# Hyena filter generation on quarters of the TensorE array, two projection weight tiles fetched at the end of the filter phase, and a signal of its own for the norm's product

## The reference

```python
hn = _rmsnorm(x, norm_mix_g[l])
proj = hn @ w_in[l]                       # columns lru_x | lru_gate | hyena v | x1 | x2
kf = _hyena_filters(seq, ...)             # two-sided filters, two orders, 512 channels
y_hy = _hyena(hy_u, ..., kf, hy_skip[l])  # two long convolutions by FFT
y_cat = concat(_rmsnorm(y_lru), _rmsnorm(y_hy)); x = x + y_cat @ w_out[l]
x = x + _hier_moe(_rmsnorm(x, norm_ffn_g[l]), ...)

def _hyena_filters(...):
    z = sin(ff1 * (feats @ fw1 + fb1)); z = sin(ff2 * (z @ fw2 + fb2))
    h = (z @ fw3).reshape(seq, 2, HY_ORDER, D_HY) * exp(-t * deltas)
    hf, hb = h[:, 0], h[:, 1]                       # forward and backward half
    k = concatenate([hf, zeros, hb[1:][::-1]])      # 4096 positions
    k = k / (sum(abs(k), axis=0) + EPS)
```

## Time and profile before

| | |
|---|---|
| median of 3 runs | 2301.02 us |
| profiled execution, its own time / its span | 2303.28 us / 2301.5 us |
| PE busy over the span | 2068.6 us (90%) |
| filter generation and transform on TensorE | about 69 to 189 us |
| next phase's first matmul | 204.35 us |

### The profile page before, as it was taken

One profiled execution on the slowest core, in us unless ns is written; L12 is line 12 of the kernel. 1 busy time (PEld: TensorE's weight loads), 2 busy tenths in 40 slices (PEclk: granted clock), 3 DMA queues, 4 the chain that ended last, 5 costly groups with the idle time before them and its releaser, 6 DMA issues. The chain is left out here.

```text
span 2301.5 us, 30650 instructions
## 1 busy us (share of the span) xinstructions
PE 2068.6 (90%) x9069; PEld 1500.0 (65%) x9070; DVE 1221.4 (53%) x1111; ACT 1115.4 (48%) x1315; POOL 345.9 (15%) x309
## 2 busy tenths in 40 slices
PE   3996999999999997878999669999999999999990
PEld 1654787786666421226878558888788788888870
DVE  7552322223666654663444475466868655664643
ACT  6762222225555532342333145466867765665643
POOL 0560000000000230220000011212111121221120
PEclk9997999999999999998999769999999999999995
DMA  5461213213111699757542356787999987886858
GB/s 190 157 226 62 64 55 92 73 37 94 39 38 38 244 341 348 273 192 249 178 165 96 128 193 196 249 275 252 374 310 375 374 293 222 297 284 207 291 145 313
DMA packets 239629, 462.08 MB, mean 201 GB/s; under 512 B 24897, under 2 KB 87461, under 8 KB 235174
## 3 DMA queue, kind: packets, MB, share of 16 engines
q1 hardware_dynamic: 201798, 375.17, 45.6%
q0 software_dynamic: 14400, 52.44, 9.5%
q10 hardware_dynamic: 23360, 33.56, 4.5%
HBM read 346.79 MB, written 114.29 MB: 200 GB/s over the span
## 5 line engine op out<-in xcount | busy, mean ns | idle before, releaser
L1762 PE MATMUL p<-wh_hi,x_hi 128*128 128x512 f32 x768 | 309.0, 402 | 1.7 <-DVE x_lo L1876 0.6
L1762 PE MATMUL p<-wh_hi,x_lo 128*128 128x512 f32 x768 | 304.4, 396 | 0.0
L1762 PE MATMUL p<-wh_lo,x_hi 128*128 128x512 f32 x768 | 304.2, 396 | 0.0
L1888 DVE TENSOR_TENSOR wh_lo<-w_raw,wh_hi 128x2048 fp32r<-128x2048 f32 x128 | 284.8, 2286 | 27.6 <-ACT wh_hi L1849 27.6
L521 PE MATMUL ps<-h_hi,wp_hi 128*128 128x512 f32 x640 | 257.7, 403 | 15.3 <-DVE wp_lo L698 15.3
L521 PE MATMUL ps<-h_lo,wp_hi 128*128 128x512 f32 x640 | 254.6, 398 | 0.0
L521 PE MATMUL ps<-h_hi,wp_lo 128*128 128x512 f32 x640 | 254.3, 397 | 0.0
L1849 ACT ACTIVATE wh_hi<-w_raw 128x2048 fp32r<-128x2048 f32 x128 | 234.8, 1924 | 0.4 <-DMA w_raw<-in_exp_w_dram 0.4
L1050 POOL TENSOR_TENSOR arena<-arena 128x512 f32<-128x512 f32 x32 | 56.9, 1778 | 762.4 <-DVE arena L1066 762.4
L1762 PEld LDWEIGHTS p<-wh_hi,x_hi 128*128 128x128 f32 x768 | 144.9, 189 | 35.6 <-issue 1.7
L1762 PEld LDWEIGHTS p<-wh_hi,x_lo 128*128 128x128 f32 x768 | 145.0, 189 | 35.2
(11 more groups left out here) (300 smaller groups left out, 3537.0 us busy)
## 6 DMA issues: line engine op xcount, KB each, us to landing
w_raw<-in_exp_w_dram SPq DMA_DIRECT2D x512, 256.0 KB, 5.9
w_raw<-in_exp_w_dram SPq DMA_DIRECT2D x128, 512.0 KB, 10.7
scratch_KA<-work SPq DMA_DIRECT2D x32, 512.0 KB, 3.0
scratch_SI<-arena SPq DMA_DIRECT2D x32, 512.0 KB, 3.4
kin<-scratch_KA SPq DMA_DIRECT2D x21, 512.0 KB, 6.1
arena<-scratch_SA SPq DMA_DIRECT2D x21, 512.0 KB, 5.1
wp_raw<-in_w_in_dram SPq DMA_DIRECT2D x20, 512.0 KB, 3.8
h_raw<-in_x_dram ACTq DMA_DIRECT2D x4, 2048.0 KB, 20.2
```

What stands on the lines that cost most here:

```text
L1762: mm = pe.matmul(acc[:, :], x[:, k, :], w, start=(k == 0 and i == 0), stop=(k == n - 1 and i == 2))
L1888: dve.tensor_tensor(lo, raw[:, j:j + 2, :], hi.bitcast(F32), ALU.subtract).then_inc(lowered, 1)
```

## The change

1. Filter generation on quarters. `zzd` (with its zero quarters) becomes `zz`, 64 rows for each half without zeros. Each generate(j) has four matmuls of 64 rows x 64 columns in place of two of 128 x 128: rows h of order o write partitions of half h for o = 0, and of the other half for o = 1. So each of the four touches another quarter of the array; the two of one order share a PSUM bank. Order 1 now has its halves swapped, so `fa` and the decay get a second version with the halves swapped; the decay tile of one j grows from 256 to 512 KB, and VectorE reads it directly instead of broadcasting one for both orders. Two memsets of `zzd` go. The skip rows of the two orders lie in different partitions, so lines 379 and 382 become two instructions of 512 elements each.
2. The first two projection weight tiles are fetched in the filter phase, as soon as the last generate is done, into the place of `zz`, ahead of the last five stores on SyncE's queue. The next block no longer fetches them, and `high(0)` and `high(1)` wait for nothing.
3. `norm_mm` is raised behind the ones-matmuls; the small matmuls raise `sums_mm`, for which only the column sums wait.

```diff
-            sp.dma_start(fa[:, :], dram["fa_filter"]).then_inc(f_in, 16)
+            sp.dma_start(fa[:, :, :], dram["fa_filter"]).then_inc(f_in, 16)
...
-                sp.dma_start(dec[:, j % 4, :], dram["decay"][:, j, :]).then_inc(dec_in[j % 4], 16)
+                sp.dma_start(dec[:, j % 4], dram["decay"][:, j]).then_inc(dec_in[j % 4], 16)
...
             sp.wait_ge(k_ready, N2 - 2)
-            sp.dma_start(skip, dram["hy_skip"]).then_inc(skip_in, 16)
+            for o in range(2):
+                sp.dma_start(skip[o], dram["hy_skip"][:, o, :]).then_inc(skip_in, 16)
+            sp.wait_ge(kgen, N2)
+            w_v = dram["w_in"].rearrange("o (k p) n -> p (o k) n", p=P)
+            for j, column in enumerate((1024, 1536)):
+                sp.dma_start(w_first[:, j], w_v[:, :, column:column + P]).then_inc(w_first_in, 16)
             for i in range(N2 - 5, N2):
                 store(i)
+            sp.wait_ge(w_first_in, 32)
...
                 for o in range(2):
-                    last = pe.matmul(pk[j % 2][:, o, :], view[:, j], w3[:, o, :], start=True, stop=True)
+                    for h in range(2):
+                        rows, out = slice(R * h, R * h + R), slice(R * (h ^ o), R * (h ^ o) + R)
+                        last = pe.matmul(pk[j % 2][out, o, :], view[rows, j], w3[rows, o, :], start=True, stop=True)
...
-                    last = pe.matmul(pa[i % 2][:, o, :], fa[:, :], tile(j)[:, o, :], start=True, stop=True)
+                    last = pe.matmul(pa[i % 2][:, o, :], fa[:, o, :], tile(j)[:, o, :], start=True, stop=True)
...
-                pe.matmul(pk[0][:, o, :], ones[:, :], acc[:, o, :], start=True, stop=True)
+                last = pe.matmul(pk[0][:, o, :], ones[:, :], acc[:, o, :], start=True, stop=True)
+            last.then_inc(norm_mm, 1)
...
-            last.then_inc(norm_mm, 1)
+            last.then_inc(sums_mm, 1)
...
-            dve.memset(zzd[R:P, 0, :], 0.0)
-            dve.memset(zzd[0:R, 1, :], 0.0)
-            dve.memset(zzd[R:P, 1, 0:1], 0.0)
+            dve.memset(zz[R:P, 0:1], 0.0)
...
-                dve.tensor_tensor(tile(j), pk[j % 2][:, :, :], dec[:, j % 4, :].unsqueeze(1).broadcast_to([P, 2, CH]), ALU.mult).then_inc(k_ready, 1)
+                dve.tensor_tensor(tile(j), pk[j % 2][:, :, :], dec[:, j % 4], ALU.mult).then_inc(k_ready, 1)
...
-            dve.scalar_tensor_tensor(out=skip, in0=pk[0][0:1, :, :], scalar=EPS, in1=skip, op0=ALU.add, op1=ALU.mult).then_inc(norm_ready, 1)
+            for o in range(2):
+                dve.scalar_tensor_tensor(out=skip[o], in0=pk[0][R * o:R * o + 1, o, :], scalar=EPS, in1=skip[o], op0=ALU.add, op1=ALU.mult).then_inc(norm_ready, 1)
...
-            load_w(0)
-            load_w(1)
...
-                act.wait_ge(w_in[j % 2], 16 * (j // 2) + 16)
-                act.activation(w_hi[:, j % 2], w_raw[:, j % 2], ACT.Copy).then_inc(w_high, 1)
+                at_least(act, w_in[j % 2], 16 * (j // 2))
+                act.activation(w_hi[:, j % 2], raw_tile(j), ACT.Copy).then_inc(w_high, 1)
```

More of the change, by code:

```diff
@@ L127, in norm_and_filters @@
         feats, z1 = work2[0:33, 0, :], work2[:, 1, :]
-        w3, fa, ones = sb("w3", [P, 2, CH]), sb("fa", [P, P]), sb("ones", [P, P])
-        dec = sb("dec", [P, 4, CH])
-        ka1, acc_flat = sb("ka1", [P, 2 * CH]), sb("acc", [P, 2 * CH])
+        w3, fa, ones = sb("w3", [P, 2, CH]), sb("fa", [P, 2, P]), sb("ones", [P, P])
+        dec = sb("dec", [P, 4, 2, CH])
         split = lambda a: a.rearrange("p (o n) -> p o n", n=CH)
@@ L134, in norm_and_filters @@
         ka, acc, kt0 = [kst[:, 3], split(ka1)], split(acc_flat), split(gain)
-        skip = dec[0:1, 0:2, :]
+        skip = [dec[R * o:R * o + 1, 0, o, :] for o in range(2)]
         pair = lambda name: ctx.enter_context(nc.psum_tensor(name, [P, 2, CH], F32))
@@ L222, in _ @@
             pe.wait_ge(mlp_sin, 3)
-            view = zzd.rearrange("p h (q l) -> p l h q", l=N2)
+            view = zz.rearrange("p (q l) -> p l q", l=N2)
             def generate(j):
@@ L236, in transform @@
                 else:
[L237 removed]
+                    pe.wait_ge(k0_ready, 2)
                 if i >= 2:
@@ L377, in _ @@
             dve.wait_ge(norm_mm, 1)
-            dve.wait_ge(skip_in, 16)
-            dve.scalar_tensor_tensor(out=skip, in0=pk[0][0:1, :, :], scalar=EPS, in1=skip, op0=ALU.add, op1=ALU.mult).then_inc(norm_ready, 1)
-            dve.wait_ge(norm_ready, 1)
+            dve.wait_ge(skip_in, 32)
+            for o in range(2):
+                dve.scalar_tensor_tensor(out=skip[o], in0=pk[0][R * o:R * o + 1, o, :], scalar=EPS, in1=skip[o], op0=ALU.add, op1=ALU.mult).then_inc(norm_ready, 1)
+            dve.wait_ge(norm_ready, 2)
             dve.wait_ge(abs_ready, 1)
-            dve.tensor_tensor(kt0[0:1, :, :], kt0[0:1, :, :], skip, ALU.add).then_inc(k0_ready, 1)
+            for o in range(2):
+                first = kt0[R * o:R * o + 1, o, :]
+                dve.tensor_tensor(first, first, skip[o], ALU.add).then_inc(k0_ready, 1)
             for i in range(NT - 2, NT):
                 low_part(i)
+            dve.wait_ge(sums_mm, 1)
             sums = pk[1][:, 0, 0:4 * CT].rearrange("p (o c two) -> p o c two", o=2, two=2)[:, :, :, 0]
@@ L401, in project_and_lru @@
         sem = PhaseSemaphores(nc, ctx)
-        marks["w_at"] = -(-nc.sbuf_base // 32) * 32
+        assert marks["w_at"] == -(-nc.sbuf_base // 32) * 32
         w_hi = sb("wp_hi", [P, 2, KC, P], F32R)
+        assert marks["w_raw_at"] == -(-nc.sbuf_base // 32) * 32
         w_lo, w_raw = in_place(nc, ctx, "wp", [P, 2, KC, P])
+        raw_tile = lambda j: (marks["w_first"] if j < 2 else w_raw)[:, j % 2]
         hraw = sb("hraw", [P, 2, 1 + SEQ + 1])
@@ L1154, in transform_tables @@
     decay = np.exp(-np.concatenate([t, back])[:, None] * deltas).reshape(N1, N2, CH)
-    out = dict(fa_filter=F, fa_signal=np.concatenate([F[:HALF], F[:HALF]]), inv_a=IA,
+    out = dict(fa_filter=np.stack([F, np.roll(F, HALF, 0)], 1), fa_signal=np.concatenate([F[:HALF], F[:HALF]]), inv_a=IA,
                fwd_b=full.reshape(N2, P, P).transpose(1, 0, 2), inv_b=inv.reshape(PAIRS, P, 2, P).transpose(1, 0, 2, 3),
-               feats=feats, decay=decay, ident=np.eye(P))
+               feats=feats, decay=np.stack([decay, np.roll(decay, HALF, 0)], 2), ident=np.eye(P))
     return {k: np.ascontiguousarray(v, dtype=f) for k, v in out.items()}
```

20 lines of the change are left out of this document (13 added, 7 removed).

## The result

| | this kernel | kernel before, same chip | ratio, 95% interval |
|---|---|---|---|
| changed kernel | 2289.24 us (2284.50 to 2289.93, 4 runs) | 2303.15 (2298.18 to 2306.78, 4 runs) | 0.9933 [0.9910, 0.9956] |
| changed kernel again (`e1_again`) | 2287.68 (2285.96 to 2288.76, 5 runs) | 2303.20 (2298.47 to 2307.77, 17 runs) | 0.9937 [0.9922, 0.9952] |

The time was forecast faster and lies inside the range (2273 to 2295), but outside the forecast's own, narrower range (2274 to 2286) in both series; the likeliest value, 2280, was 9 us too low. Some 2 us of that are the kernel before itself, which ran at 2303 here and not at 2301. The forecast gain is a ratio of 0.9909, outside both intervals. The profiled execution took 2289.61 us, with a span of 2287.8.

The account below looks back on a forecast made before the run. TensorE was taken to bound the filter loop, a chain of waits the stretch behind it. Gains of 1.5 + 13.1 + 1.4 + 0.9 + 4.1 = 21.0 us off 2303.28 gave 2282.3, 2280 as median; range 2273 to 2295.

Parts of the forecast that it names:

- first generates: Ahead of the first transform, two generates run alone and get shorter by quarters: 1.5 us won.
- loop, first transform to transform 30: Filter loop: one residue takes 2.98 us on TensorE instead of 3.43, over 29 rounds 13.1 us won.
- norm: After the loop: VectorE starts 1.75 us sooner, its four half instructions cost 0.35 us more; 1.4 us won.
- last transform, clock: Last transform: shorter TensorE idle time before it may keep the clock up; 0 or 1.9 us, taken as 0.9.
- weights: Start of the next block: ScalarE's first copy no longer waits for its weights; 4.1 us won.
- start, before the first generate: Start of the kernel: removed memsets give nothing, extra decay fetches could delay x's fourth part; taken as 0, at worst 1 us lost.
- The quarters: Generate in the loop: four quarters work at once, so eight records take two rounds, 0.858 us instead of 1.717.
- bank rival: Generate: two matmuls of one order can't share a PSUM bank, so three rounds, residue 4.70 us, time 2333; 11%.
- pair rival: Generate: quarters run only in pairs, still 1.717 us, residue 3.84 us, 5.7 us slower, time 2307; 11%.
- DMA rival: Filter loop: DMA becomes the bound, residue 3.25 us, loop gains 5.2 instead of 13.1 us, time 2288; 12%.
- store behind the new wait: End of the filter phase: stores delayed by the early weight fetch make the barrier late by up to 4 us, time 2284; 4%.
- Does anything else fill up below 2.98?: Filter loop: no other engine fills one residue's 2.98 us; ScalarE 2.59, GpSimd 2.41, VectorE 1.22 and half a split.

Follow-up runs that it names:

- e1_again: The changed kernel run once more, unchanged, for a second profile: 2287.68 us, ratio 0.9937 to the kernel before.
- e6: The changed kernel without swapping order 1's halves, so only two diagonal quarters work, with the smaller decay tiles: 2310.1 us in its one run.
- e10: The changed kernel with generates and transforms grouped by two residues and all low parts of h behind the loop: 2291.75 us in its one run.
- e9: The changed kernel with all of VectorE's low parts of h moved behind the loop: 2291.96 us in its one run.
- e7: The changed kernel with only the loop's last low part of h (tile 13) moved behind the norm: 2286.24 us, ratio 0.9914 to the kernel before.
- e3: The kernel before with only the early weight fetch and the separate norm signal, generation as before: 2297.99 us, ratio 0.9977.
- e8: The changed kernel with generates and transforms grouped by two residues, half as many changes of shape: 2288.11 us, ratio 0.9931 to the kernel before.
- e4: The changed kernel with the first decay fetches waiting until the last part of x has landed: ratio 0.9935 to the kernel before.
- e11: The changed kernel grouped by two residues, low parts behind the loop, decay fetched once for both orders (output wrong): 2289.61 us in its one run.
- e5: The kernel before run once more, unchanged, for a second profile: 2307.05 us.

## Why the prediction came out as it did

The mechanism of the main term was right, and the sum was some 6 us too high. That the time still lies inside the stated range is partly luck: the room between 2286 and 2295 was left for a full DMA and for a late store, and neither happened.

The terms, read as differences in the table (positive is time won):

```
                                          forecast  changed  e1_again
first generates                               1.5      1.6      1.6
loop, first transform to transform 30        13.1     12.3     12.3
transform 30 to the ones-matmuls (GpSimd)     0       -1.7     -1.6
norm                                          1.4      1.3      1.3
last transform, clock                         0.9      0.7      0.3
its end to the next block                     0       -0.6     -0.6
weights                                       4.1      4.3      4.3
start, before the first generate              0       -1.6     -0.2
sum at the projection's start                21.0     16.3     17.4
```

*Right.* The quarters: two rounds, and the priced change of shape with the strided load, forecast 0.41 and measured 0.43 (3.007 - 1.717 - 0.858). The loop's 0.8 us of shortfall is 3.007 against 2.98 over 29 rounds. The norm and the weights are within 0.2 us, and the parameter rows were in time. (In the norm's sum no row was given for the 0.13 us of latency; VectorE started 0.20 us behind the small matmuls, and its four instructions took 2.89 us where 2.85 were forecast.) The bank rival is refuted (e6, and the starts within 20 ns), the pair rival by the changed loop itself, and the DMA rival by e10. The DMA share came out at 0.98, not near 0.9, and still no engine waited for a transfer in the loop. The store behind the new wait: the copy did wait 2.39 us for its buffer (until 168.77), but the last transform started only at 173.39, for the norm's sake.
The Trainium skill ("TensorEngine Tiling (Array Packing)", Restrictions and Gotchas) says that different row tiles can't access one PSUM bank at the same time. The traces of the changed kernel and of e6 contradict it for row tiles that write different partitions of the bank (starts 7 ns apart, above).

Two slips in the working change nothing: 5.50 - 5.15 is 0.35, not 0.36, and the lower end of 2274 doesn't follow from the 2.4 us named for it, which give 2277.6.

*Wrong.* The step that failed is the sentence "Does anything else fill up below 2.98? ... GpSimd 2.41 ... None". The 2.41 came from a loop in which GpSimd idled 1.07 us a residue, and in that gap VectorE made its low part. The timelines of DVE and of POOL before the change:

```profile
110.13 1.25 DVE L355 TENSOR_TENSOR h_lo<-h_raw,h_hi 128x1024 fp32r<-128x1024 f32 x1
```

```profile
111.38 2.36 POOL L200 TENSOR_TENSOR acc<-acc,work 128x1024 f32<-128x1024 f32 x1 [1.08 <-ACT work L303]
```

The low part ends at 111.38, where the next addition starts. With residues 3.0 us apart the two overlap, every second addition takes about 1 us more, and GpSimd fills the new period: 2.81 us as a mean, and a gap each time. So its last additions end late, and TensorE waits 3.21 us for them; 1.7 us are lost. e9 and e7 show the cause and its size: without any low part in the loop all of the 1.7 us come back, without the last one 1.0.

The trace of before had the warning in it. At the start of its loop the two met once, and both took longer (its timelines of DVE and POOL); this one row is what lifts the mean of the earlier trace rows to 2.41 from 2.37:

```profile
82.68 1.88 DVE L355 TENSOR_TENSOR h_lo<-h_raw,h_hi 128x1024 fp32r<-128x1024 f32 x1
```

```profile
83.93 2.85 POOL L200 TENSOR_TENSOR acc<-acc,work 128x1024 f32<-128x1024 f32 x1 [0.45 <-ACT work L303]
```

The Trainium skill ("SBUF — State Buffer", Who interferes with whom) has this as a rule: a VectorE instruction with two inputs in SBUF contends with a GpSimd one that reads SBUF, while one with at most one input there does not, outside VectorE's two-port modes. This case agrees: 0.98 us more beside a low part of 1.22, and nothing beside the product with the decay, one of whose inputs is in PSUM.

The clock term came out between its ends: the last transform began at 2.4 GHz and lost it midway (3.10 us; 3.49 in e1). e3 kept it; e7 and e8 lost it earlier, though TensorE's wait in e7 was shorter than in the changed kernel. In e4 the wait was the same 3.19 us as in e1, and the ones-matmuls behind it took 3.63 us where e1's took 1.95. So the length of that wait alone doesn't decide it; what does is open.

*Not in the sum.* The way to the barrier became 0.5 to 0.6 us longer in each kernel with the new loop or the new fetches (9.06 to 9.18 us from the last copy's start, against 8.58 in both profiles of before; e9 to e11 have their low parts there). 0.4 to 0.5 of it is SyncE clearing 71 semaphores one after another, 4.53 us from the first to the last in the changed kernel instead of 4.02; why they take longer is open. Line L93 before, and in the changed kernel:

```profile
L93 SPq EVENT_SEMAPHORE_RANGE_CLEAR  x71: 25/25/30, 193.4 to 197.4; - x71
```

```profile
L93 SPq EVENT_SEMAPHORE_RANGE_CLEAR  x71: 25/30/49, 180.9 to 185.4; - x71
```

And "behind that point the instructions are the same" does not make the time the same: of the 16.3 to 17.4 us at the projection's start the profiles show 13.1 and 15.1 at the end, against a profile of before that was quick there; the medians give 13.9 and 15.5. Part is chance (e5), 1 to 3 us stay open.

## What to carry to other kernels

When the bound engine gets faster, take the durations of its neighbours from where they overlap as they will then, not from a loop in which idle time kept them apart; ask which pair of instructions will now meet. Packing the tensor array paid here only because all of its quarters work at once: two diagonal ones without zeros won nothing (e6). Each change of tile shape cost about 0.2 us, so let the same shapes follow each other. And profile the unchanged kernel a second time before explaining a loss of a few us in a phase that was not edited.

## What the runs showed of the hardware

- Four 64 x 64 float32 matmuls on four quarters start within 20 ns of each other, two of them to a PSUM bank, and the transform starts 1.09 us behind them; behind two full matmuls it started 1.72 us later. Two changes of shape and the strided load cost 0.43 us.
- A VectorE subtraction of two SBUF tiles (1.22 us) lengthens a GpSimd addition beside it from 2.37 to 3.35 us. In e8, once GpSimd has no idle time left, the subtraction itself takes up to 2.90 us.
- Of the 9 us from the last copy to the next block 4.0 to 4.5 are 71 semaphore clears, 0.057 to 0.065 us from one to the next.
- DMA engines at a share of 1.01 (368 GB/s, e10) did not slow a loop whose tiles are fetched four residues ahead.
